# A ring slot and the bias rows trade places in one buffer, and GpSimd alone splits the bias rows

## What is computed

```
gu = xb @ w_gate_up[e] + b_gate_up[e]          # 1024 -> 2048
g, u = min(gu[:, :1024], 7), clip(gu[:, 1024:], -7, 7)
hmid = (u + 1) * (g * sigmoid(1.702 * g))
y   += weight * (hmid @ w_down[e] + b_down[e])  # 1024 -> 1024
```

## Time and profile before

| | before |
|---|---|
| median of 3 runs | 1185.39 us (1185.15 to 1186.02) |
| profiled execution: span | 1185.6 us |
| profiled execution: its own time beside the span | not given apart; the span is its first to last instruction |
| TensorE matmul busy | 1117.9 us (94%) |
| VectorE / ScalarE / GpSimd busy | 319.6 / 233.6 / 36.3 us |
| DMA over the span | 445.50 MB, mean 376 GB/s |
| chain that ended last | PE 59%, DMA 35%, DVE 2%, ACT 2% |

### The profile page before, as it was taken

How to read it: one execution, slowest core, us unless ns; L and a number is a source line. 1 busy time by engine, 2 the same in 40 slices (tenths; PEclk the granted TensorE clock), 3 DMA queues, 4 the chain that set the end, 5 groups by cost and what they waited for, 6 DMA issues and landing times.

```text
span 1185.6 us, 12841 instructions
## 1 busy us (share of the span) xinstructions
PE 1117.9 (94%) x5460; PEld 498.0 (42%) x5461; DVE 319.6 (27%) x719; ACT 233.6 (20%) x460; POOL 36.3 (3%) x35
## 2 busy tenths in 40 slices
PE   8999999999999999999999998999999989999896
PEld 7887678753333333333333333333333333333332
DVE  6787665233111111221111111111111111111112
ACT  6575665341100000110010000000000000000002
POOL 0000240220000000000000000000000000000000
PEclk9999999999999999999999999999999999999999
DMA  9915336769999999999999999999999999999995
GB/s 361 353 46 185 100 143 263 273 269 426 425 426 430 426 430 426 428 426 428 426 430 427 427 428 428 427 428 426 430 427 427 428 427 428 428 427 427 428 426 215
DMA packets 44586, 445.50 MB, mean 376 GB/s; under 512 B 6096, under 2 KB 10288, under 8 KB 19728
## 3 DMA queue, kind: packets, MB, share of 16 engines
q1 hardware_dynamic: 42784, 444.38, 90.0%
q10 hardware_dynamic: 1744, 0.28, 0.1%
HBM read 443.60 MB, written 1.05 MB: 375 GB/s over the span
## 4 chain that ended last, share of the span: by engine, by line
PE 59%; DMA 35%; DVE 2%; ACT 2%; issue 0%; SPq 0%; DVEq 0%; ACTq 0%
PE ps L2074 19%; DMA R<-in_w_gate_up 16%; PE ps L2083 11%; DMA R<-in_w_down 4%; DMA MK<-in_w_gate_up 4%; PE ps L1570 4%; DMA A<-in_w_gate_up 4%; DMA XMT<-in_w_gate_up 4%; DMA XM<-in_w_gate_up 4%; PE ps L2103 4%; PE ps L2050 3%; PE ps L1590 3%; PE ps L1592 3%; PE ps L1591 3%; PE ps L1934 2%; PE ps L1826 2%
## 5 line engine op out<-in xcount | busy, mean ns | idle before, releaser
L2074 PE MATMUL ps<-R,convT 128*64 128x512 f32 x1104 | 246.4, 594 | 17.4 <-DMA R<-in_w_gate_up 17.4
L1471 DVE TENSOR_SCALAR A<-ps 128x512 f32<-128x512 f32 x30 | 20.8, 692 | 645.1 <-PE ps L2074 645.1
L2074 PEld LDWEIGHTS ps<-R,convT 128*64 128x64 f32 x1104 | 76.7, 137 | 173.7 <-issue 135.7
L2083 PE MATMUL ps<-R,A 128*64 128x512 f32 x592 | 131.9, 593 | 2.2 <-DMA R<-in_w_down 2.2
L943 ACT ACTIVATE A<-A 128x512 f32<-128x512 f32 x30 | 18.9, 631 | 470.9 <-DVE A L1471 470.9
L2083 PEld LDWEIGHTS ps<-R,A 128*64 128x64 f32 x592 | 41.5, 137 | 79.7 <-issue 75.1
L2103 PE MATMUL ps<-A,convT 64*128 64x512 f32 x248 | 61.6, 615 | 1.4 <-ACT A L950 0.7
L950 ACT COPY A<-ps 128x512 f32<-128x512 f32 x30 | 17.6, 586 | 221.3 <-PE ps L2083 221.3
L2050 PE MATMUL ps<-H,convT 128*64 128x512 f32 x256 | 60.4, 593 | 0.1
L2074 PE MATMUL ps<-XMT,convT 128*64 128x512 f32 x208 | 46.9, 593 | 2.5 <-DMA XMT<-in_w_gate_up 2.5
L2065 PE MATMUL ps<-A,convT 96*64 96x512 bf16 x192 | 32.5, 388 | 15.4 <-ACT A L948 13.7
(11 more groups left out here) (323 smaller groups left out, 1290.3 us busy)
## 6 DMA issues: line engine op xcount, KB each, us to landing
R<-in_w_gate_up SPq DMA_DIRECT2D x69, 2048.0 KB, 45.5
R<-in_w_down SPq DMA_DIRECT2D x37, 2048.0 KB, 47.1
XMT<-in_w_gate_up SPq DMA_DIRECT2D x13, 2048.0 KB, 46.0
QK<-in_w_gate_up SPq DMA_DIRECT2D x12, 2048.0 KB, 47.2
MK<-in_w_gate_up SPq DMA_DIRECT2D x12, 2048.0 KB, 47.8
A<-in_w_gate_up SPq DMA_DIRECT2D x11, 2048.0 KB, 43.1
XM<-in_w_gate_up SPq DMA_DIRECT2D x11, 2048.0 KB, 46.9
XM<-in_w_down SPq DMA_DIRECT2D x6, 2048.0 KB, 38.6
```

Source lines behind the costliest of these rows:

```text
L2074: last = mm(bank(b)[s * SLOTS:(s + 1) * SLOTS, :], xg[:, 4 * (j % 2) + 2 * c + j // 2, :], w[:, c * 2 * FF + at + s * BANK:c * 2 * FF + at ...
L2083: last = mm(bank(o)[s * SLOTS:(s + 1) * SLOTS, :], h[:, c, i * SLOTS:(i + 1) * SLOTS], w[:, c * D + s * BANK:c * D + (s + 1) * BANK], star ...
```

## The change

- The lower half of `A` becomes ring slot 4 instead of slot 7; `QK`, `XM` and `R_slot[4]` move back by one. Each slot keeps the event that it waits for, under its new fill number; the `A` slot needs no wait of its own any more, since fills 2 and 3 already wait for the last use of `w_xq`.
- The raw rows of `b_gate_up` go to `A[0:96, 5632:7680]`, those of `b_down` to `convT[0:96]`, with a semaphore each. The three loads of `b_gate_up` are now issued first, then the three of `b_down`.
- GpSimd does the whole split: for each of the two blocks (2048 and 1024 columns) cast 96 rows, subtract on 64, cast 64, subtract on 32, cast 32. All ten steps stand before its nine constants.
- ScalarE does none of the three casts. It waits for `pool_bias` 4 before `root(0)`, because the scratch area overlaps the raw rows. TensorE waits for `pool_bias` 4 before the first bias matmul.

```diff
-        ring = [R_slot[0], R_slot[2], R_slot[1], R_slot[3], QK[:, :], XM[:, :], R_slot[4], A[:, 0:4096], R_slot[5], XMT[:, :],
+        ring = [R_slot[0], R_slot[2], R_slot[1], R_slot[3], A[:, 0:4096], QK[:, :], XM[:, :], R_slot[4], R_slot[5], XMT[:, :],
...
-        b_raw = A[0:96, 0:BW]
+        b_raw = [A[0:96, 5632:5632 + 2 * FF], convT[0:96].rearrange("p c n -> p (c n)")]
...
                     if n == 2:
                         sp.wait_ge(pe_two, TWO["q", 1])
-                        for part in range(3):
-                            sp.dma_start(b_raw[part * E:(part + 1) * E, 0:2 * FF], b_gate_up[0]).then_inc(ld_bias, 16)
-                            sp.dma_start(b_raw[part * E:(part + 1) * E, 2 * FF:BW], b_down[0]).then_inc(ld_bias, 16)
-                    if n == 4:
+                        for i, src in enumerate((b_gate_up, b_down)):
+                            for part in range(3):
+                                sp.dma_start(b_raw[i][part * E:(part + 1) * E, :], src[0]).then_inc(ld_bias[i], 16)
+                    if n == 5:
                         sp.wait_ge(pe_s2, T)
-                    if n == 5:
+                    if n == 6:
                         sp.wait_ge(pe_two, TWO["oT", 1])
-                    if n == 6:
+                    if n == 7:
                         sp.wait_ge(pe_xo, 3)
-                    if n == 7:
-                        sp.wait_ge(act_part, 3)
...
-                def bias_rest(n):
-                    pool.wait_ge(act_part, 3 - n)
-                    link(nc.gpsimd.tensor_tensor(b_raw[0:n * E], b_raw[0:n * E], b_prt[0:n * E], ALU.subtract), pool_res)
-
-                bias_rest(2)
+                def bias_parts(i):
+
+                    raw = b_raw[i]
+                    prt = b_prt[:, 2 * FF * i:2 * FF * i + raw.shape[1]]
+                    pool.wait_ge(ld_bias[i], 16 * 3)
+                    link(nc.gpsimd.tensor_copy(prt, raw))
+                    for n in (2, 1):
+                        link(nc.gpsimd.tensor_tensor(raw[0:n * E], raw[0:n * E], prt[0:n * E], ALU.subtract))
+                        link(nc.gpsimd.tensor_copy(prt[0:n * E], raw[0:n * E]), pool_bias)
+
+                bias_parts(0)
+                bias_parts(1)
...
-                bias_rest(1)
...
-                act.wait_ge(ld_bias, 16 * 6)
-                nc.scalar.copy(b_prt, b_raw).then_inc(act_part, 1)
                 pv_second(1)
                 second("oT", 1, 5, last_half(oT2, 1))
-                for n in (2, 1):
-                    act.wait_ge(pool_res, 3 - n)
-                    nc.scalar.copy(b_prt[0:n * E], b_raw[0:n * E]).then_inc(act_part, 1)
+                act.wait_ge(pool_bias, 4)
...
-                pe.wait_ge(act_part, 3)
+                pe.wait_ge(pool_bias, 4)
```

More of the change, by code:

```diff
@@ L336, in trunk @@
                                                             sem("ld_xk"), sem("ld_q2"), sem("ld_o2"))
-        ld_bias, ld_end, ld_gain = sem("ld_bias"), sem("ld_end"), sem("ld_gain")
+        ld_end, ld_gain = sem("ld_end"), sem("ld_gain")
+        ld_bias = [sem("ld_bias0"), sem("ld_bias1")]
         ld_last, g_done = sem("ld_last"), sem("g_done")
@@ L341, in trunk @@
         pool_moe = sem("pool_moe")
-        act_part, pool_res = sem("act_part"), sem("pool_res")
+        pool_bias = sem("pool_bias")
         dve_seq, act_seq = sem("dve_seq"), sem("act_seq")
```

## The result

| | before | change |
|---|---|---|
| median | 1186.17 us (20 runs, 1185.15 to 1189.08) | 1188.29 us (20 runs, 1186.33 to 1193.17) |
| ratio | | 1.0022, 95% interval 1.0014 to 1.0030 |
| span of the profiled execution | 1185.6 us | 1185.9 us (its own time 1188.07) |
| median span of all executions | 1184.8 us (92) | 1186.15 us (22) |

Forecast: 1185.0, range 1183.6 to 1188.0, with 0.78 on "same". Measured: about 2.1 us slower, just outside the range. The last line counts every execution of the study. Two profiles whose spans differ by 0.3 us therefore hide a median span that is 1.35 us longer.

The account below looks back on a forecast made before the run. PE's prologue bounds the kernel to about 250 us, then a saturated DMA stream whose start sets the end. Ring -1.0 plus PE slip 0.6 gives -0.4 against 1185.39, so 1185.0 us, range 1183.6 to 1188.0.

Parts of the forecast that it names:

- GpSimd's part: GpSimd's ten-step bias split: about 23.5 us from 216.6, ending at 240, before ScalarE needs it at 251.6.
- Dear casts: GpSimd casts as slow as subtracts, 4.2 us for 2048 columns: split 34 us, ending at 251; slower case's chance 0.12.
- ScalarE's part: Three casts leaving ScalarE gain nothing; price 0 if GpSimd is done by 251.6, the latest for `root(0)`.
- The hold: VectorE's 128x4 scalings at 216.53 and 221.78 wait for GpSimd's running instruction; second only held: +1.1 us, chance 0.35.
- Nothing held: Case that 128x4 scalings are too small for GpSimd to hold: 1184.4 us, chance 0.25.
- both held: Case that GpSimd holds both scalings, with cheap casts: PE slips 2.5 us in all, 1186.9 us, chance 0.18.
- ring part: A's fill issued near 214.5 instead of 251.81 puts 4.9 us of transfer ahead; -1.0 us kept, bounds -0.3 and -1.7.
- replay: Fill issues from `R_slot[4]` to fill 11 replayed: fill 11 lands at 283.0 against 284.7, so 1.7 of 4.9 us remain.
- From 275.40 on the gap can't return: DMA stream after PE's first freed fill: PE frees six fills faster than six are brought, until 688.
- byte bound: Ring gain by bytes still queued at fill 11: through at 282.4 against 282.1 alone, so 0.3 us remain.
- landing bound: Ring gain by landing times at fill 11: 9.3 us before against 7.6 alone, so 1.7 us remain.
- PE slips 0.6: Second scaling held 1.1 us, less 0.5 slack before PE needs ScalarE's piece at 224.43: +0.6 us.

Follow-up runs that it names:

- ring alone: Changed kernel with ScalarE casting and GpSimd subtracting in turn as before, keeping the new ring order and bias-row places: 1187.01 us, ratio 1.0003.
- late split: Changed kernel with one more wait: GpSimd starts its split only when both 128x4 VectorE scalings are done: 1186.53 us, ratio 1.0002.
- second held: Changed kernel with GpSimd's split begun only when the first of the two 128x4 VectorE scalings is done: 1188.15 us, ratio 1.0019.
- no scaling: Changed kernel without the two 128x4 scalings, their factor 1/16 moved into the root of the queries: 1187.05 us, ratio 1.0005.
- delay without GpSimd: Changed kernel with GpSimd's split behind both scalings and four scalings by 1.0 ahead of the tile 1 scaling: 1188.34 us, ratio 1.0012.
- split alone: Changed kernel with the ring back in its old order, keeping the bias rows and GpSimd's split as in the change: 1187.88 us, ratio 1.0016.

## Why the prediction was wrong

Right, by its own steps:

- The views: PE bound up to 250, a saturated stream behind it, the end set by the stream's start (862.6 us from fill 15 to fill 190 in both). A's issue: forecast 214.5, measured 214.67.
- GpSimd's part: start 216.6, measured 216.67; casts 2.0 and 1.1, measured 1.89 and 1.03; subtracts 4.2 and 2.4, measured 4.06 and 2.12; end by 240, measured 238.42. "Dear casts" is out. The cast's price holds a small error: with 0.2 us of the select's 0.40 fixed, 2048 columns make 1.6 + 0.2 = 1.8 us, not 2.0; 1.89 was measured.
- ScalarE's part: `root(0)` ran at 245.83 instead of 249.78 and moved nothing.
- The hold: the second scaling is held until GpSimd's subtract ends, the first is not. PE slipped 0.31 us there (0.41 with the 0.10 from before it) for a forecast of 0.6, and 0.42 and 0.41 in the two later profiles of the change. "Nothing held" and "both held" are out; that GpSimd came second was near, 0.04 us in the first profile. The Trainium skill (SBUF — State Buffer, "Who interferes with whom") has a single-source `tensor_scalar` in a two-port mode wait for a GpSimd instruction that came first, until that one ends. The trace agrees down to 128x4, with 0.85 us instead of 0.17.

Wrong. The forecast was -0.4 us, measured +2.1. Of the 2.5 us between them 1.0 is the ring part, 0.4 the time outside the span, and 1.1 what the stall costs beyond its 0.6:

1. **The ring part, -1.0 (bounds -0.3 to -1.7), was 0.** The step that failed is the replay "with 7.6 us for a lone landing and 4.9 us between queued ones". It goes wrong at `R_slot[5]`: issued at 260.03 into an empty queue (`R_slot[4]` had landed at 259.6), it needed 8.7 us and landed at 268.7 instead of 267.2. XMT landed at 273.6 instead of 272.1, MK at 278.9 instead of 277.1, fill 11 at 286.1 instead of the 283.4 that 283.0 and the slip make, 7.2 us behind MK and not 4.9. The account by bytes closes where the replay didn't. Ahead: (279 - 229) GB/s x 42 us = 2.1 MB, the whole fill. Given back: (387 - 233) x 10 = 1.54 MB up to 262, (421 - 397) x 10 = 0.24 MB up to 272, (427 - 363) x 14 = 0.90 MB up to 286, together 2.7 MB. So more than the lead of 2.1 MB was gone by 286, a part of it because PE's events came 0.4 us later. The first item is the gap that I had seen (a wait for 259.62). The last is the one that I had not priced at all ("From 275.40 on the gap can't return"): from 272 to 286 the engines are busy for 0.94 of the time but move 363 GB/s. Both kernels have one to three fills outstanding there; one was alone in the queue for 2.6 us of the 14 in the changed kernel, for 0.5 before. That the thin queue is the reason is likely, and not shown. My byte bound (-0.3) was nearer than my landing bound (-1.7), and the middle of the two wasn't a reading of anything. The ring alone has no gain in the median either (1.0003), its fill 15 landed at 305.3 for 305.5, and the mean span without a stall is 1185.1 in the changed ring (33 executions) against 1185.0 in the old (102).
2. **No term for the time outside the span**: +0.4 us, measured in every execution of the change.
3. **"PE slips 0.6" was priced as 0.6.** What failed is the rule "every microsecond by which PE's prologue slips now goes to the end in full". A stall of 0.3 to 0.5 us cost 1.8 us in the median (change against late split). In the changed ring it goes with more executions of a low mean clock, 15 of 44 against 2 of 33. For the change this share is (8/22 - 8/92) x 2.7 us = 0.75 us of the mean. In single profiles the rule holds for the change's first (+0.41 in the issues, +0.4 in fill 15) and fails for others: +0.79 in `R_slot[4]` and +0.2 in fill 15 for its third, +0.56 and -0.1 for the second held.
4. **The base.** Span and median were set side by side as if they were the same thing; no number of the result depends on it except the forecast's absolute value, which was 0.8 us low by the three runs. On the later median the same range would have reached to 1188.8 and held the measured time, by luck: its terms would have been as wrong. And 2.1 us could be told from no change with twenty runs of each kernel, where the prediction took anything within 2.4 us for no change.

The sum over the mean of all executions: before 1186.74, change 1188.91, difference 2.2 us = 0.4 outside the span + 0.4 slip + 0.75 with low mean clocks + about 0.6 that I can't place.

Shown: the held scaling and its stall carry most of the loss (late split and no scaling bring the time back, second held keeps it, a delay without GpSimd makes a like one). Supported by counts only, and only in the changed ring: that the stall goes with a low mean clock more often. Where the clock fell is known for two of those fifteen executions: 10.2 us at the router in one, 3.4 us each at 138, 264 and 1145 in the other. Open: how a stall of 0.4 us becomes 1.8; why a stall should bear on the clock later; what cost the split alone 1.4 us with hardly a low clock; the 0.6 us; what the 0.4 us outside the span are. No kernel of the study beat the one before.

## What to carry to other kernels

Before GpSimd is given work in a stretch that was free of it, list VectorE's `tensor_scalar` instructions with SBUF operands in that stretch, however small: each can wait for the rest of a GpSimd instruction, and a tiny one on TensorE's path here cost more than its stall. A fill moved ahead of a saturated stream is worth only what keeps the queue full until the stream closes; don't reckon a nearly empty queue at the rate of a full one. And set a profiled span against other spans, never against a median of whole executions.

## What the runs showed of the hardware

- The hold is as long as what is left of the GpSimd instruction, whatever the size of the scaling: 0.85 to 1.05 us for 128x4 behind a subtract of 4.06, 1.75 behind a cast of 1.89, 3.90 behind nearly a whole subtract. Of four scalings in a row (1.90 us of cast from 215.89, subtract from 217.87) three were done at 218.03 and the fourth only at 221.96, when the subtract had ended: the gap between two GpSimd instructions isn't room for all that waits. A reciprocal of the same shape beside a GpSimd cast took 0.18 us and wasn't held, nor was any VectorE operation that reads PSUM there.
- GpSimd casts f32 to bf16 in 1.89 us for 2048 columns and 1.03 for 1024, under half of what it needs to subtract them.
- With a fill less in the queue the DMA engines moved 363 to 397 GB/s at a DMA share of 0.94 to 0.95 (262 to 286 us), against 421 to 427 at 0.99 to 1.01 in the kernel before. A 2 MB fill issued into an empty queue landed after 7.6 or 7.7 us in three cases (`XM` before and after, `R_slot[4]` after), and after 8.7 us in a fourth (`R_slot[5]` after), behind which the next was issued 4 us later.
- The same kernel, unedited, took 1189.86 us in one execution and 1185.55 in another. In the first the clock was at half for 10.2 us from 263.0, and that put the issue of fill 11 off by 4.4 us (28.34 against 23.97 behind that of `R_slot[4]`).
